# Three-layer hybrid network in split fp32: high and low parts of the weights interleaved word by word, odd buffer displaced by 128 bytes

## What is computed

```python
def conv_ffn(h, w_up, conv_w, conv_b, w_down):
    s = h.shape[1]
    u = h @ w_up
    up = jnp.pad(u, ((0, 0), (CONV_WIDTH - 1, 0), (0, 0)))
    conv = conv_b
    for j in range(CONV_WIDTH):
        conv = conv + conv_w[j] * up[:, j:j + s]
    a, g = jnp.split(conv, 2, axis=-1)
    return (jax.nn.silu(a) * g) @ w_down
...
    h = rms_norm(x, pre_mix_norm)
    proj = h @ w_in
...
    mix = jnp.concatenate([o_a, o_s], axis=-1) @ w_out
    x = x + rms_norm(mix, post_mix_norm)
```

## Time and profile before

| | |
|---|---|
| median of three runs | 2150.36 us |
| the profiled execution | 2149.57 us |
| its span from first to last instruction | 2147.8 us |
| TensorE matmuls, busy | 2098.5 us, 98% |
| weight loads, busy | 1699.6 us |
| VectorE, ScalarE, GpSimd busy | 1212.0, 906.0, 326.6 us |
| mean granted TensorE clock | 0.995 |

### The profile page before, as it was taken

The page is one execution under the profiler, slowest core; times in us unless marked ns, Lnnn a source line. Parts: engine busy times, 40 slices in busy tenths (PEclk is TensorE's granted clock), DMA queues, the critical chain, the costliest instruction groups (busy, mean ns, idle before and its releaser), DMA issues.

```text
span 2147.8 us, 26841 instructions
## 1 busy us (share of the span) xinstructions
PE 2098.5 (98%) x9776; PEld 1699.6 (79%) x9776; DVE 1212.0 (56%) x1663; ACT 906.0 (42%) x1282; POOL 326.6 (15%) x266
## 2 busy tenths in 40 slices
PE   6999999999999999999999999999999999999999
PEld 4778888878868888887766888888868878888887
DVE  5898755765366666225544566653354465666522
ACT  5883445434244444224564444442242354444411
POOL 0001221220112222001301122220000012222200
PEclk9999999999999999999999999999999999999999
DMA  7323222122212223222211232332222122222321
GB/s 235 94 75 96 82 77 71 49 69 73 95 67 94 93 96 120 95 82 67 69 40 49 89 98 98 98 114 94 86 69 88 60 73 94 98 98 97 115 95 66
DMA packets 81481, 188.96 MB, mean 88 GB/s; under 512 B 19824, under 2 KB 40432, under 8 KB 81392
## 3 DMA queue, kind: packets, MB, share of 16 engines
q1 hardware_dynamic: 81392, 187.75, 26.9%
HBM read 178.28 MB, written 9.44 MB: 87 GB/s over the span
## 4 chain that ended last, share of the span: by engine, by line
PE 92%; DVE 4%; ACT 2%; issue 1%; DMA 0%; POOL 0%; SPq 0%; DVEq 0%; ACTq 0%
PE acc L256 23%; PE acc L258 23%; PE acc L257 23%; PE bank L1248 1%; PE bank L232 1%; PE bank L1730 1%; PE bank L234 1%; PE bank L233 1%; PE acc L2636 1%; PE acc L2637 1%; PE acc L2638 1%; PE bank L2021 1%; PE bank L256 1%; PE bank L258 1%; PE bank L257 1%
## 5 line engine op out<-in xcount | busy, mean ns | idle before, releaser
L256 PE MATMUL acc<-HH,whi 128*128 128x512 f32 x1600 | 644.1, 403 | 6.8 <-DVE wlo L194 4.3
L258 PE MATMUL acc<-HH,wlo 128*128 128x512 f32 x1600 | 626.2, 391 | 0.0
L257 PE MATMUL acc<-HL,whi 128*128 128x512 f32 x1600 | 625.3, 391 | 0.0
L188 ACT ACTIVATE whi<-raw 128x1024 fp32r<-128x1024 f32 (+1 forms) x293 | 324.1, 1107 | 567.0 <-PE acc L258 537.7
L194 DVE TENSOR_TENSOR wlo<-raw,whi 128x1024 fp32r<-128x1024 f32 (+1 forms) x293 | 399.7, 1365 | 283.3 <-ACT whi L188 283.3
L256 PEld LDWEIGHTS acc<-HH,whi 128*128 128x128 f32 x1600 | 302.1, 189 | 73.8 <-DVE wlo L194 9.5
L258 PEld LDWEIGHTS acc<-HH,wlo 128*128 128x128 f32 x1600 | 301.5, 188 | 64.8
L257 PEld LDWEIGHTS acc<-HL,whi 128*128 128x128 f32 x1600 | 302.3, 189 | 62.5 <-issue 4.1
L256 PE MATMUL acc<-FH,whi 128*128 128x512 f32 x528 | 205.8, 390 | 0.0
L257 PE MATMUL acc<-FL,whi 128*128 128x512 f32 x528 | 205.4, 389 | 0.0
L258 PE MATMUL acc<-FH,wlo 128*128 128x512 f32 x528 | 205.4, 389 | 0.0
(11 more groups left out here) (393 smaller groups left out, 2666.8 us busy)
## 6 DMA issues: line engine op xcount, KB each, us to landing
raw<-w SPq DMA_DIRECT2D x257, 512.0 KB, 3.5
raw<-w SPq DMA_DIRECT2D x48, 704.0 KB, 3.9
X<-x SPq DMA_DIRECT2D x4, 512.0 KB, 5.4
x_dram<-small SPq DMA_DIRECT2D x8, 256.0 KB, 4.3
xt_dram<-small SPq DMA_DIRECT2D x8, 256.0 KB, 3.7
a_dram<-l_am SPq DMA_DIRECT2D x8, 256.0 KB, 3.4
l_xt<-xt_dram SPq DMA_DIRECT2D x8, 256.0 KB, 3.3
l_x<-x_dram SPq DMA_DIRECT2D x8, 256.0 KB, 3.2
```

Of the source, the lines that this page charges most:

```text
L188: nc.scalar.activation(hi[:, 0:kt * P], raw[u % RAW][:, 0:kt * P], ACT.Copy).then_inc(w_hi_ready, 1)
L256: nc.tensor.matmul(a[:, :], wh, tile(hi, k), start=start and k == 0, stop=False)
L257: nc.tensor.matmul(a[:, :], wh, tile(lo, k), start=False, stop=False)
L258: last = nc.tensor.matmul(a[:, :], wl, tile(hi, k), start=False, stop=stop and k == kt - 1)
```

## The change

The two parts of a weight no longer lie in two buffers. One buffer of twice the length holds them word by word: the high part of a word, then its low part. Each of the views `whi[j]` and `wlo[j]` is a slice with a step of two words over it. A 128-word weight tile thus spans 1024 bytes in place of 512, and the weight load, ScalarE's write of the high part, VectorE's read of it and its write of the low part step by 8 bytes. The buffer of even units still begins at the place within 512 bytes at which all else begins; that of odd units begins 128 bytes further. The buffers of a stage's first units and of the very first ones are interleaved too, both at the common place. `FREE`, from which everything behind is placed, comes out at the same address as before; `par`, `cst` and `small` move up by 128 bytes.

No instruction is added, removed or moved. On each of the five queues the two programs have the same instructions in the same order with the same waits, 6102 rows on TensorE's; only the names of the weight operands and the addresses differ. `busy` now reads its moving operand from the interleaved buffer with a step of one word.

```diff
+WEIGHTS_AT = (0, 128)
...
-        whi = [fixed(f"whi{j}", [P, HALF * P], F32R) for j in range(SPLIT)]
-        wlo = [fixed(f"wlo{j}", [P, HALF * P], F32R) for j in range(SPLIT)]
+        split = []
+        for shift in WEIGHTS_AT:
+            top[0] += (base_w + shift - top[0]) % LINE
+            split.append(fixed(f"split{len(split)}", [P, 2 * HALF * P], F32R))
+
+        def high_low(t, n):
+
+            return t[:, 0:2 * n:2], t[:, 1:2 * n:2]
+
+        whi, wlo = zip(*(high_low(t, HALF * P) for t in split))
...
-        first_weights = {}
+        first_weights, first_split = {}, {}
         for at0 in (0, 8, 16):
-            first_weights[at0] = [tuple(place(f"first_{n}{at0}_{j}", KD * P, FREE + (at0 + 4 * j + 2 * m) * TILE, F32R)
-                                        for m, n in enumerate(("hi", "lo"))) for j in range(2)]
+            first_split[at0] = [place(f"first{at0}_{j}", 2 * KD * P, FREE + (at0 + 4 * j) * TILE, F32R) for j in range(2)]
+            first_weights[at0] = [high_low(t, KD * P) for t in first_split[at0]]
...
-        early = [tuple(place(f"early_{n}{j}", KD * P, FREE + (24 + 4 * j + 2 * m) * TILE, F32R)
-                       for m, n in enumerate(("hi", "lo"))) for j in range(2)]
+        early = [high_low(place(f"early{j}", 2 * KD * P, FREE + (24 + 4 * j) * TILE, F32R), KD * P) for j in range(2)]
...
-            busy(c["spare"][0], c["first"][0][0], 18)
+            busy(c["spare"][0], c["first_split"][0], 18)
...
-            busy(bank[0], whi[(u0 + 11) % SPLIT], 12)
+            busy(bank[0], split[(u0 + 11) % SPLIT], 12)
```

More of the change, by code:

```diff
@@ L2691, in program @@
                 c["spare"], c["first"] = [bank[b] for b in SPARE[kind]], first_weights[at0]
+                c["first_split"] = first_split[at0]
                 stages[-2][2]["next_first"] = first_weights[at0]
```

## The result

The changed kernel takes 2188.56 us (median of 4 runs, 2187.07 to 2191.91), the kernel before 2150.79 us in the same comparison (4 runs). The ratio is 1.0175 with a 95% interval of 1.0157 to 1.0192: 38 us slower, where 80 us faster was forecast. The profiled execution has a span of 2187.8 us, 40.0 us more than before.

A forecast was written before the change was run, and what follows sets the result against it. TensorE's matmul count times the distance between starts was taken as the bound; 2149.6 - 81 (7800 x 0.93 x 11.2 ns) = 2068.6 us, 2069 at the median, 2070 with a little for stalls; range 2055 to 2205.

The forecast's parts named there:

- What bounds the kernel: On TensorE: time is the number of matmuls times the distance between their starts, 226.6 ns, plus little.
- 7800 x 0.93: Matmuls of the triples and `busy`, 7800, times the 93% taken to sit on the chain.
- the price of the weight load: Triples on TensorE: stepped loads at equal pace give 215.4 ns per matmul instead of 226.6, in all 81 us less.
- the 13.3 ns of surplus: Full-clock matmuls: 226.6 ns less 213.3 for columns, claimed to depend on how moving and next-weight reads meet.
- The two rows for equal pace: Half clock and L2502: nearest rows for equal-pace reads, at most 2.1 ns above their columns.
- The rows behind a break: Stream after a break: 232 ns, then 226.7, with the same loads; taken to show the surplus is no fixed fee.
- The number on the chain: Matmuls of L256 to L258 on the chain: some 6540 of 7032, 93%.
- the splits at nothing: ScalarE's write, 1.06 us, and VectorE's subtraction, 1.23 us per unit: stepping was taken to cost nothing.
- The bound above: Splits twice as long, one word per two: 4.6 us per unit, still in time; 21 us at nine uncovered places.
- the slower one: Rival: weight load pays for memory opened; doubled span gives 240 ns per matmul, +96 us, 2247; chance 0.32.
- Its milder size: Slower case with one of the two buffer places spared: 2198; chance 0.14 for slower at or below 2205.
- The rival of a fixed fee: The 13.3 ns belong to TensorE's fp32r weight change whatever the addresses: no difference, 2150; chance 0.08.

## Why the prediction was wrong

**What bounds the kernel** was read rightly: the time is the number of matmuls times their distance, in both kernels. The distances of the triples under 300 ns, first ones of each unit included, have a mean of 227.3 ns before (some 7330 of them) and 232.9 ns after (some 7350). 5.5 ns on the 7800 x 0.93 matmuls of the prediction's own count are 40 us, the 40.0 us of the span. The windows alone would give 6 to 7 ns. The difference is the slow stretches behind breaks. Within ten matmuls of one the mean went from 230.3 to 232.6 ns; further on it went from 226.7 to 232.9.

**The step that failed** is the price of the weight load: it was set at 215.4 ns per matmul, 11.2 ns less than before, and 5.5 ns more than before were measured. It rested on the reading that the 13.3 ns of surplus are meetings of two reads that sweep past each other at unequal pace. The runs contradict it twice. A load that stays on one word and sweeps nothing still has 230.3 ns. Loads with the step that was to make the pace equal have 230 to 234 ns at each of six places. That a stepped load does keep equal pace was worked out from L825 (whose starts lie 111.6 ns apart in the trace; 110 was the length of the piece over 32), and no run shows it. The record has the load at 188 ns without the step and 196 with it. The two rows for equal pace, the half clock and L2502, were no models for a full-rate stream: in both the moving operand was needed at half the rate, and that, not the equal pace, may be what relieves them.

**The rows behind a break** were read the wrong way round. 232 ns was taken for a disturbance of a stream whose own distance is 226.7, and as proof that the surplus depends on how the reads meet. It does, but the runs fit the reverse: 230 to 235 ns is the ordinary level (of the places and steps tried, only nil and 256 bytes without a step lie well below it, and just below lie 192 bytes with 229.1 ns and, in some stretches, the one-word loads with 228.8), and 226.7 is a settled state. The stream reaches it some ten matmuls behind a break, and holds it where each load reads words in a row and starts at the moving operand's place modulo 256 bytes; at 16 bytes a few units reach it too. The change took the first condition away from even units, by the step, and both from odd ones, by the step and by the 128 bytes. The two losses do not add up: 6.5 ns for the step at nil, 5.6 ns for the 128 bytes without a step, 4.7 ns for both. That 226.7 is a settled beat is an inference from these patterns. For it speak the few units 16 bytes behind that fell into it, and the one-word loads, which hold 228.8 ns in one stretch and 230.7 in another. A steady beat is not by itself the fast one: the loads interleaved at nil hold 233 to 234 ns as evenly as the kernel of before its 226 to 227, while at other places the distances repeat in groups of two to seven, between 226 and 241 ns. The mechanism inside TensorE was not shown.

**The number on the chain** (93%) fits the 40.0 us, and **the splits at nothing** were right: ScalarE's 7% lie beneath 551 us of its waiting. The bound above, splits twice as long, was the right fear for a step of four words: there the cover is gone, and most of the 149 us beside the 59 of the distance are lost in waits for the splits and for the taps behind them on VectorE. How they divide was not tested. **The rivals**: the slower one had the right sign and the wrong mechanism. It charged the surplus to the memory opened, 240 ns at a doubled span; measured were 232.9, and the one-word load refutes it. Its milder size, 2198 with one place spared, came near 2189 for another reason; so it is luck, and not the mechanism, that the measured time lies inside the stated range. The rival of a fixed fee is half alive: in no kernel was the mean of either parity below 226.7 ns, at any address or step tried. Whether the 13.3 ns that remain are a fee for changing fp32r weights at the full clock stays open, since no run had a stream without weight loads. The Trainium skill's figure of 215.7 ns (TensorE: Matmul & The Clock Gate, Part 2) was reached by none of these streams, and its statement that loading the next weights takes no read bandwidth from the running matmul is hard to bring together with them: the load's address alone changes the distance by 6.5 ns.

No version tried beats the kernel of before by more than the measurement can tell.

## What to carry to other kernels

Where fp32r matmuls run back to back with a weight load each, give the stationary tile unit step and the moving operand's address modulo 256 bytes; in this kernel that is worth 6 ns in 227, near 2% of the time, and a displacement of one word is enough to lose it. A distance that falls to its best value only after some matmuls without a break is a state to be kept, not a baseline to be improved: ask what it needs before changing a layout. And before a mechanism is made out of a case at half the rate, look for one at the full rate, and until then keep the opposite sign well inside the range.

## What the runs showed that was not expected

The distance depends on the load's start in relation to the moving operand with a period of 256 bytes: 226.9 at nil, 232.5 at 4 bytes, 232.8 at 16, 233.4 at 32 and 64, 232.5 at 128, 229.1 at 192, 233.2 at 224 and 227.0 ns at 256. At 128 bytes one displaced load in three lengthens the matmul beside which it runs and the one after (227, 232, 234 ns); at 4 bytes it lengthens all three (233, 232, 235). The same loads can hold different steady distances in different stretches of one execution: 228.6 and 230.7 ns for one word read 128 times. Whether ScalarE and VectorE write with a step changes neither value (226.9 and 232.5 ns with and without). A step of two words costs ScalarE 7% and VectorE nothing. With a step of four the weight load is 313 ns long, longer than the 235.1 ns from one matmul to the next.
